# Hybrid decoder layer with a top-4-of-32 MoE on one core: the order of the first expert passes, of their routing, and of the last store of the head

## Chip, core and metric

One core of one Trainium2 chip. The metric is the device time of one execution in microseconds (us), median over the timed runs.

## What is computed

A decoder layer for 512 prompt tokens and 8 sample tokens (520 rows of 1,024), in fp32: attention and a pooling mixer with their projections, then a mixture of experts. The part that matters here:

```python
logits = (h @ w_router + b_router)
topv, topi = lax.top_k(logits, TOP_K)          # 4 of 32
gates = jax.nn.softmax(topv, axis=-1)
# per expert, for the tokens that chose it:
gu = xb @ w1[e] + b1[e]                        # 1024 x 2048
gate, up = gu[:, :D_FF], gu[:, D_FF:]
gate = jnp.minimum(gate, SWIGLU_LIMIT)
up = jnp.clip(up, -SWIGLU_LIMIT, SWIGLU_LIMIT)
act = (up + 1) * (gate * jax.nn.sigmoid(SWIGLU_ALPHA * gate))
out = act @ w2[e] + b2[e]                      # 1024 x 1024
# out * gate is added to the token's row; y = x + gate_ffn * sum
```

All 32 experts are used, so all of w1 and w2 (32 x 12 MB) pass from HBM once.

## The kernel before, in words

**Two parts.** `head` (L399) computes the mixers, the norm, the router's logits, the four choices of each token, each token's place in its experts' lists (`posm`) and the gates (`found`). A barrier of all engines (L358) ends it. `experts` (L1666) then runs 32 *passes*, one expert each, with a class from `ORDER` (L49): A handles 256 tokens, B 128, C 64, D 32. Experts are given to passes by rank of their token counts; passes 0 and 1 are pinned to experts 0 and 1 (class C), so that their weights can be loaded before ranking is known. What does not fit is left to *extra passes* at the end. A and B split fp32 into a high part (ScalarE, L1958) and a low part (VectorE, L2138), with three products each; C and D use fp32 products on 64- or 32-column tiles of the array.

**Weight units and the ring.** A pass has 12 units of 1 MB: 8 of the first matrix, u = 0 to 7 ("up"), 4 of the second, u = 8 to 11 ("down"). SyncE loads units in the order `LOADS` (L89) into a ring of 13 slots (`RING`), and units (1,1) to (1,4), the *early* units, to places of their own. From the 14th load on, each waits until TensorE has used (`unit_used`) the unit that had the slot (L1773). `pe_order` (L74) gives TensorE's order: up of pass 0, down of 0, up of 1, up of 2, down of 1, up of 3, down of 2 and so on; in an A pass the down of the pass before comes after four ups. `LOADS` is the same order without the early units, pass 0 first.

**Rows of a pass.** For pass p: GpSimd copies the expert's columns (`pick_static`, L1817 and L1818), VectorE compares them with slot numbers (`one_hot`, L2070 or L2066), TensorE multiplies (`find_slots`, five small bf16 products into bank 6), VectorE makes the indices (`indices`, L2089 to L2093), GpSimd gathers rows of h by indirect DMA (L1841), TensorE turns them (`turn_rows`, L2331, bank 6), ScalarE copies them out (L1912). In steady state this is done one to three passes ahead.

**Start of the experts.** VectorE's program is: one-hot and indices of pass 0, `gates` (L2208 to L2214), `ranks` (L2166 to L2174, which gives the experts of passes 2 to 31 as `eid`), memsets, one-hot and indices of pass 1, one-hot of pass 2, `extra_passes` (L2178 to L2202), then the passes. GpSimd waits for `eid` before it copies the columns of passes 1, 2 and 3, and gathers pass 1's rows after that. TensorE turns the rows of pass 1 after pass 0's up units, then the activations of pass 0, then `down(0)`. After an up, VectorE clamps banks 0 and 1 (L2100, L2102; `gu_free`) before TensorE may write the biases of the next up.

**End of the head.** Tiles are handled in the order 0, 1, 2, samples (TP), 3. For each, h is stored to DRAM (SyncE L626 for the first three, ScalarE L954 for the last two), turned by TensorE (`turn_h2`, L1606), multiplied with the router (L1616), and VectorE picks the four experts. TensorE waits for tile 3's h before `turn_h2(3)`. SyncE loads units (0,7) to (0,10) once the output projection is done (`xo_ready`), then (1,0) and (1,1); it ends with a wait for all stores of h (L640), and the barrier waits for it. The rest of the early units is loaded by `experts`.

Touched, by line: `pe_order` L74, `SLOT` L90, `behind` L338, SyncE's loads L631 to L637, TensorE's end of the head L1651 to L1664, SyncE's ring wait L1767, GpSimd's start L1859 to L1869, ScalarE's and VectorE's loops over passes, TensorE's `find_slots`, `turn_rows` and its loop.

## Time and profile before

| | us |
|---|---|
| median of 3 runs (1419.0 to 1425.48) | 1425.12 |
| the profiled execution | 1425.26 |
| its span, first to last instruction | 1423.7 |
| TensorE busy (matmul) | 1239.1 (87%) |
| VectorE busy | 668.5 (47%) |
| ScalarE busy | 490.2 (34%) |
| GpSimd busy | 216.3 (15%) |
| DMA: 481.23 MB, mean over the span | 338 GB/s |

All times of rows are us from the span's start. A slice of the page is 35.6 us. The granted clock of TensorE (PEclk) is 1.00 at 2.4 GHz and 0.50 at 1.2 GHz. The DMA share is the mean busy share of the core's 16 DMA engines; it can read slightly over 1. A C unit is 8 matmul records (4 products), and a busy matmul record's end is modelled, so starts are the better measure.

### The profile page before, as it was taken

Reading aid. Unit: us, or ns where it says so; the run is one execution under the profiler, and the core shown is the slowest. Engines: PE = TensorE matmul, PEld = TensorE weight load, DVE = VectorE, ACT = ScalarE, POOL = GpSimd, SP = SyncE. Lnnn points to the kernel's source line nnn. Section 1 sums busy time; section 2 is a strip of 40 time slices with the busy share of each in tenths; the row PEclk is TensorE's granted clock in tenths of the full one; section 3 lists DMA queues with packets and bytes.
Section 4 is the critical chain, followed back from the end, with each engine's and each line's share of the span. In section 5 each row is a group of like instructions: output and inputs, shape, how many; then the busy total and the mean of one; then the engine's idle time right before and its main releaser. Section 6 shows DMA issues by size and latency. Waiting matters only on the chain.

```text
span 1423.7 us, 17364 instructions
## 1 busy us (share of the span) xinstructions
PE 1239.1 (87%) x6405; PEld 729.7 (51%) x6405; DVE 668.5 (47%) x969; ACT 490.2 (34%) x703; POOL 216.3 (15%) x285
## 2 busy tenths in 40 slices
PE   5798777986899998899899969999879999999771
PEld 2353435542267564666575427556447555647330
DVE  2531562355378564353585225427334435848313
ACT  5010431231156443233464213225323333727310
POOL 2211321021101111110211102011201021101001
PEclk9799878996999999899999999999989999999975
DMA  9940585438889999999999999999999999999994
GB/s 289 383 119 5 192 286 201 173 128 324 334 309 390 375 403 397 392 396 355 376 411 406 403 391 396 395 354 405 404 388 405 367 346 408 407 410 405 413 393 187
DMA packets 113657, 481.23 MB, mean 338 GB/s; under 512 B 12497, under 2 KB 13824, under 8 KB 83820
## 3 DMA queue, kind: packets, MB, share of 16 engines
q1 hardware_dynamic: 100460, 451.52, 80.3%
q0 software_dynamic: 12768, 27.47, 7.3%
q8 instruction: 52, 0.85, 0.2%
q10 hardware_dynamic: 344, 1.12, 0.2%
q14 instruction: 33, 0.27, 0.0%
HBM read 463.46 MB, written 24.14 MB: 343 GB/s over the span
## 4 chain that ended last, share of the span: by engine, by line
PE 51%; DMA 13%; SPq 5%; DVE 5%; issue 2%; ACT 1%; POOLq 0%; DVEq 0%; ACTq 0%
PE bank L2305 49%; DMA raw<-in_w 10%; SPq L525 3%; DVE rawr L2138 1%; PE bank L2354 1%; DMA yd<-ost,slot_tok 1%; DMA yd<-gu,slot_tok 1%; SPq L531 1%; PE bank L2331 1%; ACT hi L1958 1%; SPq L535 1%; DVE gu L2102 1%; DVE gu L2100 0%; DVE yf L2298 0%; DVE yf L2295 0%
## 5 line engine op out<-in xcount | busy, mean ns | idle before, releaser
L2138 DVE TENSOR_TENSOR rawr<-raw,hi 128x1024 fp32r<-128x1024 f32 x288 | 341.2, 1220 | 137.7 <-ACT hi L1958 134.7
L1958 ACT CAST hi<-raw 128x1024 fp32r<-128x1024 f32 x288 | 295.2, 1049 | 167.0 <-PE bank L2305 117.5
L2305 PE MATMUL bank<-raw,xT_even 128*64 128x512 f32 (+1 forms) x704 | 139.5, 615 | 4.9 <-DMA raw<-in_w 4.9
L2305 PE MATMUL bank<-raw,aT 128*32 128x256 f32 (+1 forms) x992 | 116.4, 485 | 15.4 <-DMA raw<-in_w 15.4
L1853 POOL DMA_INDIRECT yd<-ost,slot_tok x31 | 54.4, 1754 | 356.3 <-ACT ost L1941 356.0
L2305 PE MATMUL bank<-raw,xT_odd 128*32 128x512 f32 (+1 forms) x544 | 88.6, 677 | 21.5 <-DMA raw<-in_w 21.5
L2305 PE MATMUL bank<-hi,xTh_even 128*128 128x512 f32 x256 | 85.1, 415 | 7.5 <-DVE rawr L2138 7.5
L2305 PE MATMUL bank<-hi,aTh 128*128 128x512 f32 x240 | 77.5, 405 | 9.7 <-DVE rawr L2138 9.7
L2305 PEld LDWEIGHTS bank<-raw,aT 128*32 128x32 f32 (+1 forms) x992 | 42.3, 126 | 79.3 <-issue 41.7
L2305 PE MATMUL bank<-rawr,xTh_even 128*128 128x512 f32 x256 | 81.7, 401 | 0.0
L2305 PE MATMUL bank<-hi,xTl_even 128*128 128x512 f32 x256 | 81.2, 399 | 0.0
L2305 PE MATMUL bank<-hi,xTh_odd 128*128 128x512 f32 x224 | 73.2, 408 | 7.0 <-DVE rawr L2138 7.0
L2305 PE MATMUL bank<-rawr,aTh 128*128 128x512 f32 x240 | 76.0, 399 | 0.0
L2305 PE MATMUL bank<-hi,aTl 128*128 128x512 f32 x240 | 75.6, 397 | 0.0
L1926 ACT ACTIVATE gu<-gu 128x512 f32<-128x512 f32 (+1 forms) x50 | 29.1, 583 | 134.9 <-DVE gu L2100 134.9
L2100 DVE TENSOR_SCALAR gu<-bank 128x512 f32<-128x512 f32 (+1 forms) x50 | 31.3, 627 | 94.0 <-PE bank L2305 94.0
L2305 PEld LDWEIGHTS bank<-raw,xT_even 128*64 128x64 f32 (+1 forms) x704 | 35.7, 128 | 69.7 <-issue 58.9
L2305 PE MATMUL bank<-rawr,xTh_odd 128*128 128x512 f32 x224 | 70.2, 395 | 0.0
L2305 PE MATMUL bank<-hi,xTl_odd 128*128 128x512 f32 x224 | 69.9, 394 | 0.0
L2156 DVE SCALAR_TENSOR_TENSOR aTl<-bank,aTh 128x512 fp32r<-128x512 f32 x30 | 20.7, 689 | 100.6 <-ACT aTh L1919 100.6
L1941 ACT ACTIVATE ost<-bank,slot_gate 128x512 f32<-128x512 f32 (+1 forms) x43 | 26.0, 633 | 120.9 <-PE bank L2305 107.6
L2089 DVE TENSOR_REDUCE slot_raw<-bank 128x1 f32<-128x2 f32 (+1 forms) x32 | 5.0, 156 | 126.4 <-PE bank L2305 125.4
(358 smaller groups left out, 1730.1 us busy)
## 6 DMA issues: line engine op xcount, KB each, us to landing
raw<-in_w SPq DMA_DIRECT2D x356, 1024.0 KB, 17.4
raw<-in_w_ada SPq DMA_DIRECT2D x24, 1024.0 KB, 6.0
raw<-in_w SPq DMA_DIRECT2D x48, 512.0 KB, 11.5
w_in_sb<-in_w_in SPq DMA_DIRECT2D x1, 5120.0 KB
w_out_sb<-in_w_out SPq DMA_DIRECT2D x4, 1024.0 KB, 6.2
early<-in_w SPq DMA_DIRECT2D x4, 1024.0 KB, 8.3
xs<-in_x_prompt SPq DMA_DIRECT2D x4, 512.0 KB, 15.7
yd<-zero POOLq DMA_DIRECT2D x4, 512.0 KB, 10.9
```

Source lines behind the costliest of these rows:

```text
L525: sp.dma_start(raw.rearrange("p (k n) -> p k n", k=2), src).then_inc(landed, 16)
L531: sp.dma_start(raw[:, kk * D:(kk + 1) * D].rearrange("p (h c) -> p h c", h=2), src[:, :, j * 512:(j + 1) * 512]).then_inc(landed, 16)
L535: sp.dma_start(raw, src).then_inc(landed, 16)
L1853: gp.indirect_dma_start(yd_of[n], bass.IndirectOffsetOnAxis(ap=m.slot_tok[:, p % 6, b:b + 1], axis=0), out_rows(p, b), None, bounds_check= ...
L1926: nc.scalar.activation(gate, gate, ACT.Silu, scale=ALPHA).then_inc(silu_ready, 1)
L1941: done = nc.scalar.activation(out_rows(p, b)[:, n * w:(n + 1) * w], src, ACT.Copy, scale=m.slot_gate[:, p % 6, b:b + 1])
L1958: nc.scalar.copy(m.hi[:, (2 * n + h) % HI, :], m.raw[:, slot, h * D:(h + 1) * D]).then_inc(hi_done, 1)
L2100: v.tensor_scalar(gate, g, LIMIT, None, ALU.min).then_inc(gmin_ready, 1)
L2102: v.tensor_scalar(up, u, LIMIT, -LIMIT, ALU.min, ALU.max).then_inc(gu_free, 1)
L2138: v.tensor_tensor(m.rawr[slot][:, half], m.raw[:, slot, half], m.hi[:, (2 * n + h) % HI, :].bitcast(F32), ALU.subtract).then_inc(lo_done, 1)
L2156: v.scalar_tensor_tensor(m.aTl[:, k:k + n, :].rearrange("p k n -> p (k n)"), bank[7][:, 0:n * P], 1.0 / ALPHA, m.aTh[:, k:k + n, :].bitcas ...
L2305: return nc.tensor.matmul(out, lhsT, rhs, start=start, stop=stop, skip_group_check=True)
```

## The change

`pe_order` changes for the first passes: up of 0, up of 1, down of 0, up of 2, down of 1. The order of loads stays; a slot is now freed in TensorE's order (`FREED`), so that the 14th to 25th loads wait for other units than before. Pass 1 becomes an ordinary pass in all programs: pass 0's activations are turned within it, and the search of pass 2 moves to after pass 0's third unit, the rows of pass 1 to after its fifth. GpSimd picks the columns of pass 1, whose expert is known, gathers its rows and loads its biases ahead of the wait for `eid`. VectorE makes one-hot and indices of pass 1 ahead of `ranks`, with half of a memset, and does `extra_passes` in pass 6; its buffer `behind` moves. TensorE does 9 products of the identity with itself after the search of pass 1 and 20 before `turn_h2(3)`; both go to banks that nothing reads. SyncE loads (0,9) and (0,10) only when tile 3's h has been turned, which is after ScalarE has issued its last stores.

```diff
--- before.py
+++ after.py
@@ -76,18 +76,19 @@
     units = []
     for p in range(NE + 1):
         up = [(p, u) for u in range(W1_UNITS)] if p < NE else []
-        down = [(p - 1, u) for u in range(W1_UNITS, UNITS)] if p > 1 else []
-        if not p:
-            down = [(0, u) for u in range(W1_UNITS, UNITS)]
+        down = [(p - 1, u) for u in range(W1_UNITS, UNITS)] if p else []
         cut = 4 if p < NE and ORDER[p] == "A" else W1_UNITS
-        units += up[:cut] + down + up[cut:] if p else up + down
+        units += up[:cut] + down + up[cut:]
     return units
 
 
 USED = {unit: n + 1 for n, unit in enumerate(pe_order())}
 EARLY = [(1, u) for u in range(1, 5)]
 LOADS = [(0, u) for u in range(UNITS)] + [unit for unit in pe_order() if unit[0] and unit not in EARLY]
-SLOT = {unit: n % RING for n, unit in enumerate(LOADS)}
+FREED = [unit for unit in pe_order() if unit not in EARLY]
+SLOT = {unit: n for n, unit in enumerate(LOADS[:RING])}
+for after, unit in zip(FREED, LOADS[RING:]):
+    SLOT[unit] = SLOT[after]
 ALL_USED = NE * UNITS
 SPLIT_UNITS = [unit for unit in pe_order() if ORDER[unit[0]] in SPLIT]
 NTH = {unit: n for n, unit in enumerate(SPLIT_UNITS)}
@@ -335,7 +336,7 @@
         m.eid = ot("eid", [P, NE + EXTRAS + 1], I32)
         m.warm = ot("warm", [P, 1])
         m.cmp = at("cmp", [P, NE, NE], F32, aT0)
-        m.behind = at("behind", [P, EXTRAS, NE], F32, aT0)
+        m.behind = at("behind", [P, EXTRAS, NE], F32, x0 + KC * P * 4)
         m.begun = at("begun", [P, EXTRAS, NE], F32, aT0 + 4096)
         m.yf = at("yf", [P, TP, D], F32, raw0)
         m.yfs = at("yfs", [D // NS // 2, P], F32, raw0 + TP * 4096)
@@ -629,11 +630,13 @@
             for t in TURN[:3]:
                 store_rows(t)
             sp.wait_ge(s.xo_ready, TT)
-            for u in range(7, UNITS - 1):
+            for u in range(7, 9):
+                load_unit(sp, 0, 0, u)
+            sp.wait_ge(s.h2_tr, 2 * TT)
+            for u in range(9, UNITS - 1):
                 load_unit(sp, 0, 0, u)
             sp.wait_ge(m.x1_out, 3 * 16)
             load_unit(sp, 1, 1, 0)
-            sp.wait_ge(s.h2_ready, TT)
             load_unit(sp, 1, *EARLY[0])
             sp.wait_ge(s.ulast_out, 16)
             sp.wait_ge(h2_free[0], 3 * 16)
@@ -1653,6 +1656,8 @@
             positions(1)
             positions(2)
             router(TP)
+            for _ in range(20):
+                mm(bank[4][:, 0:P], m.ident[:], m.ident[:], start=True, stop=True)
             turn_h2(3)
             positions(TP)
             router(3)
@@ -1764,7 +1769,7 @@
                 if p >= PINNED and not u:
                     e[p] = sp.value_load(m.eid[0:1, p:p + 1], min_val=0, max_val=NE - 1)
                 if n >= RING:
-                    sp.wait_ge(unit_used, USED[LOADS[n - RING]])
+                    sp.wait_ge(unit_used, USED[FREED[n - RING]])
                 m.load_unit(sp, e[p], p, u)
 
             def load_extra(x):
@@ -1859,13 +1864,16 @@
             bias(0)
             gp.wait_ge(xg_init, 1)
             gather(0)
+            gp.wait_ge(gates_ready, 1)
+            experts_of[1] = 1
+            pick(1, 1)
+            gp.wait_ge(xg_init, 2)
+            gather(1)
+            bias(1)
             gp.wait_ge(eid_ready, 1)
-            gp.wait_ge(gates_ready, 1)
-            for p in range(1, 4):
+            for p in range(2, 4):
                 pick_static(p)
             gp.wait_ge(xg_init, 3)
-            gather(1)
-            bias(1)
             for p in range(NE + 2):
                 if p:
                     bias(p + 1)
@@ -1996,24 +2004,15 @@
                         swish(c, h, HB[p])
                     continue
                 high_to(USED[p, 1] + 2)
-                if p > 1:
-                    last_act(p - 1, 0)
+                last_act(p - 1, 0)
                 high_to(USED[p, 3] + 2)
-                if p > 1:
-                    last_act(p - 1, 1)
+                last_act(p - 1, 1)
                 for g in range(4):
                     high_to(USED[p, 4 + g] + 2)
-                    if p:
-                        static_x(p + 1, g)
-                if not p:
-                    static_x(1, 0)
+                    static_x(p + 1, g)
                 for h in range(HALVES[c]):
                     swish(c, h, HB[p])
-                if not p:
-                    last_act(0, 0)
-                    last_act(0, 1)
-                    gated(0)
-                if p > 1:
+                if p:
                     high_to(USED[p - 1, UNITS - 1] + 2)
                     gated(p - 1)
             last_act(NE - 1, 0)
@@ -2217,16 +2216,16 @@
             v.memset(m.xg[0][:, 0, 0:512], 0.0).then_inc(xg_init, 1)
             indices(0)
             gates()
+            v.memset(m.xg[1][:, 0, 0:512], 0.0).then_inc(xg_init, 1)
             v.wait_ge(i_done, 2)
             v.tensor_reduce(m.slot_gate[:, 0, 0:1], bank[6][:, 8:11].unsqueeze(1), AX_X, ALU.add).then_inc(gates_ready, 1)
+            one_hot(1)
+            indices(1)
             ranks()
-            v.memset(m.xg[1][:], 0.0).then_inc(xg_init, 1)
+            v.memset(m.xg[1][:, 0, 512:D], 0.0)
             v.memset(m.xg[0][:, 0, 512:D], 0.0)
             v.memset(m.xg[0][:, 1, :], 0.0).then_inc(xg_init, 1)
-            one_hot(1)
-            indices(1)
             one_hot(2)
-            extra_passes()
             for p in range(NE):
                 c = ORDER[p]
                 if c == "A":
@@ -2248,26 +2247,20 @@
                     swiglu(p, 2, USED[p, 7])
                     continue
                 low_to(USED[p, 1] + 2)
-                if p > 1:
-                    last_act(p - 1, 0)
+                last_act(p - 1, 0)
                 low_to(USED[p, 2] + 1)
                 indices(p + 2)
                 low_to(USED[p, 3] + 1)
-                if p > 1:
-                    last_act(p - 1, 1)
+                last_act(p - 1, 1)
                 low_to(USED[p, 4] + 1)
                 for g in range(4):
                     low_to(USED[p, 4 + g] + 1)
-                    if p:
-                        low_x(p + 1, g)
+                    low_x(p + 1, g)
                     if not g:
                         one_hot(p + 3)
-                if not p:
-                    low_x(1, 0)
                 swiglu(p, 0, USED[p, 7])
-                if not p:
-                    last_act(0, 0)
-                    last_act(0, 1)
+                if p == ORDER.index("A") - 2:
+                    extra_passes()
             low_to(ALL_USED)
             last_act(NE - 1, 0)
             last_act(NE - 1, 1)
@@ -2316,11 +2309,9 @@
 
                 if p < NE:
                     pe.wait_ge(oh_ready, p + 1)
-                    if p:
-                        pe.wait_ge(x_ev, HB[max(p - 1, 1)])
-                        pe.wait_ge(xl_done, SB[max(p - 1, 1)])
-                    if p == 2:
-                        pe.wait_ge(idx_ready, 2)
+                    if p > 1:
+                        pe.wait_ge(x_ev, HB[p - 1])
+                        pe.wait_ge(xl_done, SB[p - 1])
                     find(ORDER[p], m.pb[:, p % 4] if p else m.found[:, 0], 5 if p else 2)
 
             def turn_x(c, g, xg):
@@ -2336,7 +2327,7 @@
                 if p < NE and g < HALVES[ORDER[p]]:
                     if not g:
                         pe.wait_ge(xg_in[p % 2], GATHERED[p])
-                        pe.wait_ge(idx_ready, min(p + 2, NE) if p else 1)
+                        pe.wait_ge(idx_ready, min(p + 2, NE))
                     else:
                         pe.wait_ge(x_ev, HB[p] + g)
                         if ORDER[p] in SPLIT:
@@ -2501,9 +2492,14 @@
                     last = mm(bank[6][:, 8:11], m.oh[:, t, 0:P], m.found[:, 0, t, 2:5], start=not t, stop=t == TP)
                 last.then_inc(i_done, 1)
 
+            def keep_busy(n):
+                for _ in range(n):
+                    mm(bank[7][:, 0:P], m.ident[:], m.ident[:], start=True, stop=True)
+
             find_slots(0)
             find_gates()
-            pe.wait_ge(gates_ready, 2)
+            find_slots(1)
+            keep_busy(9)
             turn_rows(0, 0)
             for p in range(NE):
                 c = ORDER[p]
@@ -2537,22 +2533,15 @@
                     continue
                 for u in range(W1_UNITS):
                     up_static(p, u)
-                    if u == 1 and p > 1:
+                    if u == 1:
                         turn_last_act(p - 1, 0)
-                    if u == 3 and p > 1:
+                    if u == 3:
                         turn_last_act(p - 1, 1)
                     if u == 2:
-                        find_slots(p + 2 if p else 1)
-                    if u == 4 and not p:
-                        find_slots(2)
-                    if u >= 4 and p:
+                        find_slots(p + 2)
+                    if u >= 4:
                         turn_rows(p + 1, u - 4)
-                if not p:
-                    turn_rows(1, 0)
-                    turn_last_act(0, 0)
-                    turn_last_act(0, 1)
-                    down(0)
-                elif p > 1:
+                if p:
                     down(p - 1)
             turn_last_act(NE - 1, 0)
             turn_last_act(NE - 1, 1)
```

## Rows read from the trace of the kernel before

**Rows 1.** The page's slices (40 of 35.6 us), DMA busy in tenths.

```profile
DMA  9940585438889999999999999999999999999994
```

**Rows 2.** Windows: stretch, length, busy us by engine, TensorE clock, DMA share, GB/s.

```profile
338.00:348.00 10.00, 8.89 (x28) 3.35 (x30) 4.99 (x7) 0.58 (x1) 2.32 (x6) 0.60 0.29 100
348.00:366.00 18.00, 12.07 (x65) 4.35 (x61) 13.81 (x38) 1.78 (x3) 4.72 (x8) 0.92 1.01 416
366.00:374.00 8.00, 8.00 (x29) 2.59 (x31) 0.00 (x0) 0.00 (x0) 0.00 (x0) 0.76 0.60 226
384.00:403.00 19.00, 17.28 (x66) 9.77 (x63) 11.00 (x12) 8.61 (x10) 2.04 (x3) 0.82 0.67 230
403.00:480.00 77.00, 75.61 (x352) 50.37 (x352) 53.29 (x63) 42.50 (x50) 9.79 (x11) 1.00 0.98 365
```

**Rows 3.** SyncE's timeline, 344 to 352: its first loads into the ring after the wait.

```profile
344.99 6.56 SPq L535 DMA_DIRECT2D raw<-in_w  x4
```

**Rows 4.** Timeline of TensorE, 318 to 400: start, length, group, [idle before it].

```profile
318.32 1.97 PE L1606 MATMUL bank<-ident,h 128*128 128x128 f32 x8 [4.67 <-DVE h L1302]
320.96 3.62 PE L1616 MATMUL bank<-w_router_sb,h2T 128*128 128x32 f32 x16 [0.57 <-ACT h2T L947]
339.11 1.08 PE L2331 MATMUL bank<-ident,xg_even 128*128 128x128 f32 x4 [5.83 <-issue]
340.12 1.22 PE L2305 MATMUL bank<-bt,sel_sb 12*128 12x512 f32 x2
341.27 7.66 PE L2305 MATMUL bank<-raw,xT_even 128*64 128x512 f32 x24
361.41 0.63 PE L2331 MATMUL bank<-ident,xg_odd 128*128 128x128 f32 x4 [3.17 <-DVE slot_tok L2093]
381.38 3.65 PE L2305 MATMUL bank<-early,xT_odd 128*64 128x512 f32 x16
393.37 1.74 PE L2305 MATMUL bank<-bt,sel_row 12*128 12x512 f32 x4 [1.72 <-DVE gu L2102]
```

**Rows 5.** Timeline of TensorE, 296 to 319, at the full clock.

```profile
298.10 5.40 PE L1582 MATMUL bank<-w_out_sb,mixT 128*128 128x512 f32 x12
303.33 1.04 PE L1606 MATMUL bank<-ident,h 128*128 128x128 f32 x8
307.64 1.87 PE L1616 MATMUL bank<-w_router_sb,h2T 128*128 128x32 f32 x16
```

**Rows 6.** VectorE's last step of the head; SyncE's wait; stores of h (KB, us to landing).

```profile
327.23 0.21 DVE L1279 RECIPROCAL gsum<-gsum 8x1 f32<-8x1 f32 x2
SPq L640 <- DMA h2d<-h: 8.5, 1, 8.5
h2d<-h SPq DMA_DIRECT2D x3, 512.0 KB, 5.7
h2d<-h ACTq DMA_DIRECT2D x1, 512.0 KB, 8.9
```

**Rows 7.** Timelines of VectorE and GpSimd, 339 to 361.

```profile
339.89 0.18 DVE L2174 CAST eid<-ex 128x32 int32<-128x32 f32 x1
342.67 0.76 DVE L2070 TENSOR_TENSOR oh<-pcol,rows_sb 128x640 bf16<-128x640 f32 x1
350.27 0.09 DVE L2178 MEMSET zero_e<- 128x32 f32 x1
360.79 0.15 DVE L2202 CAST eid<-ends 128x1 int32<-128x1 f32 x1
341.90 1.57 POOL L1817 COPY pcol<-posm 128x5 f32 x1 [0.47 <-issue]
```

**Rows 8.** TensorE's waits, 560 to 582 (us, times, longest); VectorE's timeline in pass 6.

```profile
PE bank L2305 <- DMA raw<-in_w: 7.2, 6, 1.9
PE bank L2305 <- DVE rawr L2138: 2.0, 1, 2.0
544.07 4.62 DVE L2138 TENSOR_TENSOR rawr<-raw,hi 128x1024 fp32r<-128x1024 f32 x4
```


## Prediction

> **What bounds the kernel now.** Read the slices first: DMA is at nine tenths or more in nearly all of the expert phase [rows 1]; 1 MB weight units (1.05 million bytes) come at 416 GB/s in an undisturbed stretch, 2.52 us each [rows 2]. So the end is set by when the weight stream starts and by every stretch in which it stands still before the passes that wait for weights; where TensorE itself waits again, at 560 to 582 us, six of its waits, 7.2 us, are for weights [rows 8]. Then read the stage windows for those still stretches [rows 2]: width times (1 minus share) gives 7.1 us at 338 to 348, 3.2 at 366 to 374, 6.3 at 384 to 403, and 1.5 over 403 to 480. The first is the wait for the first use of a weight: the ring of 13 slots and the 4 early units are full, and the first load after them is issued at 344.99, when unit (0,0) has been used [rows 3]. The others are a full ring too, since TensorE is what stops: it uses a C unit in 1.8 us (two units, 16 records, in 3.65), faster than weights come, but sits idle 3.2 us for the rows of pass 1, whose indices stand behind the extra-pass arithmetic in VectorE's program, then turns the activations and restarts cold [rows 4, 7].
>
> **The sum**, against the profiled execution's 1425.26 us (span 1423.7; the median of the runs is 1425.12, practically the same).
>
> *1. End of the head.* Tile 3's chain is transposes 1.97 us and router 3.62 us, both at the half clock [rows 4]; at full clock the same groups take 1.04 and 1.87 [rows 5]. The 20 identity products stand in the 4.67 us in front [rows 4]. No row shows a 128-column fp32 product. Bounds: 0.23 us (router, 32 columns, 1.87/8) and 0.90 (512 columns, 5.40/6) [rows 5]; I take 0.24, nearest the narrow one, so 20 take 4.8 us, about the wait. If they hold the clock, 0.9 + 1.75 = 2.7 us go; at 0.37 each they run 2.7 us over and the gain is nil. The expert phase starts only when tile 3's store has landed, too: SyncE waits 8.5 us for it, it lands 8.9 us after its issue at 318.3, the first three in 5.7 [rows 6]. The store now has two weight units ahead of it in place of five: I take 5.7, landing at 324.0. VectorE's last step moves from 327.4 [rows 6] to 324.7; both are early enough, so 2.7 us. If the store kept 8.9 it would land at 327.2 and the gain would be 0.2. The Trainium skill (DMA: Bandwidth & Descriptors, Queues, rings and completion order) says that each DMA engine takes turns between queues packet by packet. ScalarE's queue would then not stand behind SyncE's weights at all, the reordering would free nothing, and with 0.2 here the sum below would be 2.5 higher; 8.9 beside 5.7 speaks against that. The delayed units, (0,9) and (0,10), leave DMA idle some 2 us at 318; they aren't used before pass 0's second matrix, and the stream of the first 17 units then ends near 340.5 rather than 339.1.
>
> *2. First use.* TensorE turns pass 0's rows at 339.11 after 5.83 us of idleness [rows 4]; the landing shifts by 2.7, to 336.4. Into the idle stretch go pass 1's copies, one-hot (0.76 us [rows 7]) and search, some 1.9 us together, then 9 products, at the cold router's 0.45 each (3.62/8) 4.1 us: 6.0 against 5.83. So they cost nearly nothing by themselves; at twice that price they would be 4 us late and take all of this step. If the clock is up, the transposes and biases lose about half of 1.08 and 1.22 us, on the path 0.8, and the first three units, 7.66 us where 5.5 would do, lose 1.9 in unit (0,0). First use: 344.99 - 2.7 - 2.7 = 339.6 warm, 342.3 cold. I take 340.6, one late, since GpSimd's copy for pass 1 now runs beside a memset, and such a copy took 1.57 us [rows 7]. [...] The stream restarts **4.4 us** earlier (2.7 to 5.4).
>
> *3. Between pass 0 and pass 1.* The extra-pass arithmetic (350.27 to 360.9 [rows 7]) leaves the path, and pass 0's second matrix goes behind pass 1's first. Early units free no slot, so the tenth load after the restart waits for unit (1,5). TensorE from first use to there: 13 units at 1.8 = 23.4, three groups of transposes at 0.63 = 1.9, two searches of five small products, an estimate of 0.2 each beside the 0.63 of four transposes, = 0.4, biases 0.6, and a new wait: pass 1's biases need VectorE's two limits of pass 0, 1.7 us by the row of the same wait before pass 2 [rows 4]. Queued behind it are all of pass 1's units; SyncE waits for those. Sum 28.0 us. DMA in that time: 9 units at 2.52 (416 GB/s) and pass 2's rows (0.5 MB, 1.3 us): 24.0. Still stretch: 4.0 us. Then 7 units (17.6 us) are freed by TensorE in 6 units and biases, some 13 us, so none before pass 2. That replaces 3.2 + 6.3 = 9.5: **5.5 us** gained. If the clock falls in the 1.7 us wait, two units at the half clock take 3.6 of it.
>
> *4. Passes 2 and 3.* From unit (2,0) on both kernels free and load in the same order. The DMA now has a backlog of 2 to 4 us there: of 1.5 idle I take **1.2**, between 0 and 1.5.
>
> *5. Hidden.* Ranking ended at 340.1 [rows 7] and moves behind one-hot and indices of pass 1, some 1.7 us, and forward by 2.7: 339.1; three memsets (1.9 us) and pass 2's one-hot follow by 342, and its search is due after three units, at 344. GpSimd's bias and gather of pass 1 only move forward. SyncE's first expert-dependent load is the fourth after the ring. The extra-pass work, 10.6 us, now stands in pass 6 ahead of VectorE's last four low halves at 544.07 [rows 8]: unit (5,10) waits some 9.9 us. Behind it TensorE has 7.2 us of waits for weights and 2.0 for VectorE that can shrink [rows 8], plus the 2 to 5 us by which it leads DMA more than before. Cost taken: none.
>
> Sum: 4.4 + 5.5 + 1.2 = 11.1; 1425.3 - 11.1 = **1414.2 us**.
>
> **Rivals.**
> *A, the clock stays down at both places:* the first use is 2 us earlier, the still stretch is 4.0 + 3.6 = 7.6, and nothing is left for passes 2 and 3: 2.0 + 1.9 + 0 = 3.9, so **1421.4**. For: the half clock lasted through the transposes and biases after 339.11. Against: the wait in the head is nearly filled.
> *B, partly given back:* the pass 6 wait restarts TensorE cold, 9.9 + 3.6 = 13.5, against 9.2 of waits to absorb it; 4.3 reaches pass 8, which then ends later with a full ring: 1414.2 + 4.3 = **1418.5**.
> *C, slower:* the same place, if nothing of the 13.5 is absorbed because weights of pass 7 and the A pass stop behind a full ring, with A's 3.9 as the only gain: 1425.3 + 13.5 - 3.9 = **1434.9**. It decides from the point where the A pass starts over 4 us late (A) or over 11 (forecast). Against: weights are what TensorE waits for behind this place, and an empty ring of 13 units is 33 us of transfer.
> *D, the change doesn't do what it says:* pass 1's rows or pass 2's slots come late and TensorE stops after unit (0,2) or (0,3). The margin is 2 us; 5 us late, 3 over it, makes **1417.2**.
>
> **How the numbers follow.** Forecast 0.68, A 0.13, B 0.09, D 0.05, C 0.05. Best bounds together: 5.4 + 7.2 (a new wait hidden) + 1.5 = 14.1, 1411.2; the runs of before spread over 6 us, so the low end goes 3 further, to 1408. The high end takes in D, B and A: 1421.5. About 0.5%, 7 us, is what a measurement here can tell from none: faster needs under 1418.0. The forecast and D are faster: 0.73; A and B are the same: 0.22; C is slower: 0.05.
>
> **What would show it.** Expert phase about 2.7 us earlier, router(3) near 1.9 us; first load after the ring near 340.6; no transposes of pass 1 after pass 0 but within it; still stretches of DMA near 340 and 365, of 2 and 4 us, and none at 395; VectorE's extra-pass steps in pass 6 with TensorE idle up to 10 us beside them. Wrong if the still stretches after the restart stay near 9.5 us, or if those of the A passes (640 to 700) grow by what was won.

## The result

| | before | after |
|---|---|---|
| median of 4 runs, us | 1422.06 (1417.87 to 1425.48) | 1406.34 (1398.94 to 1407.76) |
| profiled execution, us | 1425.26 | 1407.76 |
| its span, us | 1423.7 | 1406.1 |

The ratio is 0.9886, 95% interval 0.9857 to 0.9914: faster by 1.1%. The direction and the places are those of the prediction; the size is not: 15.7 us by the medians (17.6 by the spans of the two profiles) against 11.1 forecast. The median lies 1.7 us below the range's low end, 1408; that it lies outside hangs on the base as well, since the kernel before has a median of 1422.06 here and the forecast counted from 1425.3: the same 15.7 us taken off that would be 1409.6, inside.

To compare profiles one needs a common start, since unchanged code ahead of the change shifts from one execution to the next. I count from SyncE's issue of unit (0,7), just ahead of the first thing that the change moves. Here it is in SyncE's timeline of the kernel before, then of the kernel after (start us, us over which the group was issued, line, operation, count):

```profile
311.34 0.33 SPq L535 DMA_DIRECT2D raw<-in_w  x1
```

```profile
309.76 0.33 SPq L536 DMA_DIRECT2D raw<-in_w  x1
```

So 1.6 us of the profiles' difference were there before the change begins. From here on, "at 28.5" means 28.5 us behind this issue.

**The head.** TensorE's timeline of the kernel after (start us, us, group, idle before it), the answer to [rows 4] up to the barrier:

```profile
312.01 4.73 PE L1660 MATMUL bank<-ident 128*128 128x128 f32 x40
318.79 2.15 PE L1619 MATMUL bank<-w_router_sb,h2T 128*128 128x32 f32 x16
```

The 20 products (40 records) took 4.73 us, 0.24 each, and fill the old wait of 4.67 us; transposes (1.09) and router take 3.2 us in place of 5.6. VectorE ends the head at 323.80; its first step of the experts, with the wait for the barrier ahead of it:

```profile
325.52 0.83 DVE L2069 TENSOR_TENSOR oh<-posm,rows_sb 128x640 bf16<-128x640 f32 x1 [1.71 <-PEq L359]
```

**The first use.** TensorE again, from the nine products to the wait between the passes:

```profile
330.81 3.81 PE L2298 MATMUL bank<-ident 128*128 128x128 f32 x18
334.84 0.66 PE L2322 MATMUL bank<-ident,xg_even 128*128 128x128 f32 x4 [0.22 <-DMA xg_even<-h2d,slot_tok]
336.23 5.37 PE L2298 MATMUL bank<-raw,xT_even 128*64 128x512 f32 x24
352.77 0.69 PE L2298 MATMUL bank<-bt,sel_sb 12*128 12x512 f32 x2 [1.48 <-DVE gu L2101]
353.39 2.57 PE L2298 MATMUL bank<-raw,xT_odd 128*64 128x512 f32 x8
355.74 3.00 PE L2298 MATMUL bank<-early,xT_odd 128*64 128x512 f32 x8
```

The rows land 0.22 us after the nine products end, transposes and the first three units run at the full clock (5.37 where [rows 4] has 7.66), and TensorE doesn't stop until pass 1's biases, where it waits 1.48 us for VectorE's limits. Behind that wait the clock does fall (0.73 granted at 352.7 to 359): two units take 5.57 us, where at the full clock they take 3.83 (e9 below).

SyncE's timeline of the kernel after: the first load into a freed slot, and the load into the slot that unit (2,0) frees:

```profile
338.21 32.20 SPq L536 DMA_DIRECT2D raw<-in_w  x11
...
383.31 0.35 SPq L536 DMA_DIRECT2D raw<-in_w  x1
```

The first is at 28.5 against 33.7 before [rows 3], 5.2 us earlier. The same two of the kernel before are at 344.99 [rows 3] and here:

```profile
400.70 3.15 SPq L535 DMA_DIRECT2D raw<-in_w  x2
```

That is 89.4 behind the issue of (0,7) before, and 73.5 after: **15.8 us earlier**, practically the whole gain of the medians (the best bounds of the prediction together made 14.1).

**The DMA.** Windows of the kernel after (stretch, length, busy us by engine, clock, DMA share, GB/s), the answer to [rows 2]:

```profile
338.00:350.00 12.00, 12.00 (x63) 4.17 (x61) 3.70 (x8) 0.58 (x1) 4.08 (x10) 1.00 1.00 391
360.00:373.00 13.00, 13.00 (x66) 4.41 (x64) 3.81 (x8) 1.78 (x4) 1.32 (x2) 1.00 0.72 268
373.00:384.00 11.00, 11.00 (x51) 5.63 (x48) 6.38 (x6) 6.36 (x8) 2.31 (x4) 1.00 0.97 388
384.00:403.00 19.00, 18.43 (x91) 14.65 (x90) 15.49 (x18) 12.21 (x14) 1.80 (x1) 1.00 1.02 416
403.00:480.00 77.00, 76.18 (x346) 48.03 (x344) 54.65 (x63) 44.28 (x50) 8.56 (x11) 1.00 1.00 386
```

The 7.1 us at 338 to 348 are gone, one still stretch (width times 1 minus share, as in the prediction) of 13 x 0.28 = 3.6 us is left at 360 to 373 (4.0 forecast), and the one at 384 to 403 is gone. Summed as in the prediction, the kernel before stood still 11.0 us from its first load to 480, this one 3.9 (3.6 and 11 x 0.03): 7.1 less, and the forecast said 6.7. By this measure the prediction was right; yet the load freed by (2,0) gained 15.8 - 5.2 = 10.6 us over the same stretch. The measure is what has to be looked at.

**Pass 6.** TensorE's waits of the kernel after, 500 to 600 (us, times, longest), against [rows 8]:

```profile
PE bank L2298 <- DVE rawr L2137: 9.6, 1, 9.6
```

The extra-pass arithmetic costs a wait of 9.6 us (9.9 forecast), and all the waits for weights, 7.2 us before, are gone.

### The profile page after: what moved, and what is told of

Its sections match the earlier page's. It is cut to its first block, busy times and chain, and to the rows that moved or that the text cites. A ratio compares the mean times of both kernels' runs of the same rounds, so it can differ in the third digit from the quotient of the medians.

```text
span 1406.1 us, 17471 instructions
## 1 busy us (share of the span) xinstructions
PE 1237.9 (88%) x6463; PEld 732.5 (52%) x6463; DVE 670.0 (48%) x970; ACT 490.2 (35%) x703; POOL 215.4 (15%) x285
## 4 chain that ended last, share of the span: by engine, by line
PE 54%; DMA 12%; DVE 5%; SPq 3%; issue 1%; ACT 1%; POOLq 0%; ACTq 0%; DVEq 0%
PE bank L2298 51%; DMA raw<-in_w 9%; SPq L526 3%; DVE rawr L2137 2%; PE bank L2345 1%; DMA yd<-ost,slot_tok 1%; PE bank L2322 1%; DMA yd<-gu,slot_tok 1%; ACT hi L1966 1%; DVE gu L2101 1%; SPq L532 1%; DMA xg_even<-h2d,slot_tok 0%; DVE gu L2099 0%; DVE yf L2291 0%; DVE yf L2288 0%
## 5 line engine op out<-in xcount | busy, mean ns | idle before, releaser
L2298 PE MATMUL bank<-hi,aTh 128*128 128x512 f32 x240 | 78.5, 409 | 17.8 <-DVE rawr L2137 17.8
L2298 PEld LDWEIGHTS bank<-hi,aTh 128*128 128x128 f32 x240 | 45.1, 194 | 33.8 <-DVE rawr L2137 22.5
## 6 DMA issues: line engine op xcount, KB each, us to landing
yd<-zero POOLq DMA_DIRECT2D x4, 512.0 KB, 10.6
```

The lines of the kernel that those rows point to most:

```text
L2298: return nc.tensor.matmul(out, lhsT, rhs, start=start, stop=stop, skip_group_check=True)
```

## The experiments

Two theories. **Theory 1:** what counts is the time that TensorE itself takes up to a point where the ring is full and the DMA waits for it, first unit (2,0); what the DMA did before is forgotten there. **Theory 2**, the prediction's measure: the DMA's still stretches add up to the end. Two of the expectations name a Theory 3 too: the passes of class A take up about 4 us of any delay, and what is over goes through to the end. The table gives for every kernel the ratio of its time to the kernel before's, and from its one profile the issue of the load freed by (2,0) and the time at which the DMA has moved 100 MB since the issue of (0,7), both counted from that issue. A single profile's end scatters by some 4 us either way after that, so positions in the stream tell more than ends.

| kernel | ratio (95%) | (2,0) | 100 MB |
|---|---|---|---|
| before | 1 | 89.4 | 275.9 |
| after | 0.9886 (0.9857 to 0.9914) | 73.5 | 259.7 |
| f1, before + the order | 0.9978 (0.9954 to 1.0003) | 84.1 | 270.1 |
| f2, after - the order | 0.9928 (0.9904 to 0.9951) | 81.9 | 268.1 |
| e4, extra passes ahead | 0.9953 (0.9926 to 0.998) | 81.3 | 267.2 |
| e3, extra passes in pass 1 | 0.9886 (0.9858 to 0.9913) | 73.7 | 259.7 |
| e1, no products | 0.9889 (0.9864 to 0.9914) | 77.4 | 263.2 |
| e9, no twenty | 0.9881 (0.9848 to 0.9914) | 74.1 | 260.0 |
| e10, no nine | 0.9882 (0.9849 to 0.9915) | 74.8 | 260.7 |
| e2, old store order | 0.9885 (0.9859 to 0.991) | 74.7 | 260.7 |
| g1, ring loads late | 0.9884 (0.985 to 0.9918) | 73.8 | 259.8 |
| e6, 15 products before pass 2 | 0.9889 (0.9865 to 0.9912) | 75.4 | 261.6 |
| e12, 40 products before pass 2 | 0.9939 (0.9913 to 0.9966) | 81.0 | 267.3 |
| h1, 40 products before pass 4 | 0.9945 (0.9921 to 0.9969) | 73.7 | 267.8 |
| g2, 6 products, extras in pass 1 | 0.9887 (0.986 to 0.9915) | 73.2 | 259.6 |
| h2, 6 products | 0.9859 (0.9825 to 0.9893) | 72.0 | 258.4 |

In fifteen of the sixteen the two columns differ by 185.8 to 186.6 us; the one exception is h1, which delays TensorE between them.

### Which part brings it

f1 is the kernel before with the new order of units and slots alone, f2 the changed kernel with the old order, everything else kept.

```diff
-        down = [(p - 1, u) for u in range(W1_UNITS, UNITS)] if p > 1 else []
-        if not p:
-            down = [(0, u) for u in range(W1_UNITS, UNITS)]
+        down = [(p - 1, u) for u in range(W1_UNITS, UNITS)] if p else []
...
-        units += up[:cut] + down + up[cut:] if p else up + down
+        units += up[:cut] + down + up[cut:]
...
-                    sp.wait_ge(unit_used, USED[LOADS[n - RING]])
+                    sp.wait_ge(unit_used, USED[FREED[n - RING]])
```

> The kernel before with the new order of units and slots alone (up 0, up 1, down 0); rows of pass 1, extra passes, store and clock as before. Theory 1 (TensorE's time at the first unit of pass 2 carries to the end): TensorE still stops for rows and activations after pass 0, but the wait and the half clock ahead of pass 2 (1.7 us and about 3 us) go: the load freed by (2,0) 4 to 6 us earlier than before, and the end too: ratio 0.996 to 0.997. Theory 2 (DMA's still stretches): the tenth load now waits for (1,5), some 12 us of stillness in place of 11 in several pieces: ratio 0.999 to 1.002.

> The kernel before with everything of the change except the order of units: products, store, rows of pass 1 ahead of ranking, extra passes in pass 6. Theory 1: first load of the ring 5 to 6 us earlier counted from the issue of (0,7), the 3.2 us wait for rows gone, most of the half clock after it too, so the load freed by (2,0) 11 to 13 us earlier, and the end with it: ratio 0.991 to 0.992. Theory 2 (my sum by still stretches: 4.4 us for the start, 3 for the rows): 7 to 8 us, ratio 0.9945 to 0.995.

The order alone moves (2,0) by 5.3 us, everything but the order by 7.4; together 15.8. That is 3.1 us more than the two, but it doesn't show that they exist only with both. f2 has the changed kernel's TensorE program up to the first units, and its profile has them at the half clock (0.50 granted from 329.8 to 339; the changed kernel is at the full clock from 334 on). TensorE's timeline of f2, pass 0's first three units:

```profile
336.05 7.00 PE L2314 MATMUL bank<-raw,xT_even 128*64 128x512 f32 x24
```

They take 5.37 in the changed kernel. So f2's first load into a freed slot comes at 31.1 instead of 28.5, 2.7 us late by the clock alone. With these given back f2 moves (2,0) by some 10.1 us (an estimate), and the two parts practically add up. The times agree: f2's ratio of 0.9928 is 10.2 us, and its profiled execution is 4 us above its median. Neither expectation of f2 came as it stood. Its position, 7.4 us, is theory 2's number (theory 1 had 11 to 13), its ratio lies between the two theories' ratios, and the interval reaches both. f1's position lies in theory 1's 4 to 6 us, while its interval reaches both theories' ratios. These two runs split the change, then, and don't decide between the theories.

TensorE's waits of f1 between 341 and 394 say why the order alone gets so little:

```profile
PE bank L2331 <- DVE slot_tok L2093: 3.2, 1, 3.2
PE bank L2354 <- DVE gu L2109: 2.1, 1, 2.1
```

The rows of pass 1 are still late and pass 0's activations are still turned at once. The extra passes weigh about as much as the order, which f2 lacks (8.4 us later than the changed kernel at (2,0), 2.7 of them clock). e4 puts them back ahead of pass 0 in VectorE's program, e3 puts them into pass 1:

```diff
             one_hot(2)
+            extra_passes()
...
-                if p == ORDER.index("A") - 2:
-                    extra_passes()
```

> The changed kernel with the extra-pass arithmetic back ahead of pass 0's work on VectorE. Indices of pass 2 come 10 us later, TensorE waits some 6 to 7 us for them inside pass 0 and loses clock; the 9.6 us wait in pass 6 goes. Theory 1: the load freed by (2,0) 7 us later than in the changed kernel, end 7 us later, ratio 0.9935. Theory 3: 3 to 4 us later, ratio 0.991. Theory 2: DMA has loads queued during that wait for pass 0's freed slots only, still stretch of 3 to 5 us more, ratio 0.991 to 0.992.

> The changed kernel with the extra-pass arithmetic in pass 1, where VectorE is idle for 8 us, in place of pass 6. Theory 1: the 9.6 us wait of TensorE in pass 6 goes, TensorE then waits for weights in pass 7 instead, and the A pass starts no more than 1 us earlier, so the end is within 1 us of the changed kernel (ratio 0.988 to 0.9886). Rival B of the prediction (part of the wait reached the A pass): 2 to 5 us faster, ratio 0.985 to 0.987.

The longest of e4's waits of TensorE, 338 to 393:

```profile
PE bank L2321 <- DVE slot_tok L2092: 6.3, 1, 6.3
```

The indices of a pass come 6.3 us late and (2,0) is 7.7 later, near theory 1's 7; the ratio is 0.9953 (0.9935 forecast, inside the interval). In e3 nothing of the early stream changes, and TensorE's main waits at 500 to 600 are these:

```profile
PE bank L2298 <- DMA raw<-in_w: 5.0, 5, 1.9
PE bank L2298 <- DVE rawr L2137: 2.5, 1, 2.5
```

Without the 9.6 us wait TensorE simply waits for weights again, the ratio is the same 0.9886, and 100 MB arrive at the same 259.7. The wait in pass 6 costs nothing that these runs can see: shown, not only argued. What no run leaves out by itself is the early picking of pass 1's rows, so its share of the gain isn't known.

### The head

e1 leaves out all 29 products, e9 the 20, e10 the nine; e2 loads (0,9) and (0,10) again with (0,7), ahead of the last store:

```diff
-            for _ in range(20):
-                mm(bank[4][:, 0:P], m.ident[:], m.ident[:], start=True, stop=True)
...
-            keep_busy(9)
```

```diff
-            for u in range(7, 9):
-                load_unit(sp, 0, 0, u)
-            sp.wait_ge(s.h2_tr, 2 * TT)
-            for u in range(9, UNITS - 1):
+            for u in range(7, UNITS - 1):
                 load_unit(sp, 0, 0, u)
...
             load_unit(sp, 1, 1, 0)
+            sp.wait_ge(s.h2_ready, TT)
             load_unit(sp, 1, *EARLY[0])
```

The last lines bring back the old wait of unit (1,1) for tile 3's h, so that it too is loaded as before.

> The changed kernel without its 29 identity products. Theory 1 (TensorE's time at the first unit of pass 2 passes whole to the end): the head ends about 1.5 to 2 us later after the issue of unit (0,7), the first load of the ring 4 to 5 us later (half clock in transposes, biases and unit (0,0)), the load that unit (2,0) frees as much later, and so the end: about 5 us slower than the changed kernel, ratio to the kernel before 0.992. Theory 2 (only DMA's still stretches count, as I predicted): the still stretch at the first use grows by 3 to 4 us and the one in pass 1 stays, so 3 to 4 us slower, ratio 0.991; the two differ in whether the end moves as much as the load freed by (2,0).

> Without the 20 products ahead of the rows' transposes, with the nine kept. Theory 1: transposes and router run at half clock again, the first operation of the experts comes 2.1 us later behind the issue of unit (0,7) (17.8 instead of 15.7), the load freed by (2,0) at 76 instead of 73.5, ratio 0.990. Rival: the nine alone suffice (the head has slack elsewhere): issue at 73.5, ratio 0.9886.

> Without the nine products ahead of the first pass, with the twenty kept. Theory 1: the first two expert units run at half clock, the first load into a freed slot comes 2.8 us later, the load freed by (2,0) at 76.3 instead of 73.5, ratio 0.9905. Rival: the clock holds from the router's work across the wait, or the loss is taken up in the wait between passes 0 and 1: issue at 73.5, ratio 0.9886.

> The changed kernel with units (0,9) and (0,10) loaded with (0,7) again, ahead of the last store. Theory 1 (the store's landing holds the barrier): h lands some 2.5 us later, about 8.5 us after its issue, the barrier moves from VectorE's last step to that landing, 2 to 2.5 us later, and the end with it: ratio 0.990. Rival (queues take turns packet by packet, so the weights of the other queue hardly matter): the landing moves by under 0.5 us and so does the end: ratio 0.9886.

The barrier lets the experts start at 15.8 in the changed kernel, at 17.8 without the twenty (e1, e9), at 17.8 with the old order of the store (e2), and at 17.8 before. Either part alone gives nothing there: each removes one of two things that end at nearly the same time. The store itself, in the DMA issues of 300 to 340 of the changed kernel and then of e2 (KB, us from issue to landing):

```profile
h2d<-h ACTq DMA_DIRECT2D x1, 512.0 KB, 3.0
```

```profile
h2d<-h ACTq DMA_DIRECT2D x1, 512.0 KB, 8.9
```

The time to landing is 3.0 us with two weight units issued ahead of it and 8.9 with five ([rows 6] has 8.9 too). The forecast took 5.7. The two units were in fact through: in either kernel the DMA moves 2.1 to 2.2 MB from the issue of (0,7) to that of the store, which is two units. In the changed kernel the DMA is half idle then (share 0.55 at 316.7 to 318.5), in e2 it isn't (1.06): three of the five units are still to come, and the store lands only when the DMA has moved 3.4 MB more, about these three and the store.

Yet none of the four loses more than 3.8 us at (2,0): e9 0.6, e10 1.2, e2 1.1, e1 3.8, where the expectations of e9 and e10 had 2.5 to 2.8 each. e9's units behind the wait between the passes show where it goes:

```profile
357.91 0.70 PE L2296 MATMUL bank<-bt,sel_sb 12*128 12x512 f32 x2 [1.48 <-DVE gu L2099]
358.54 1.94 PE L2296 MATMUL bank<-raw,xT_odd 128*64 128x512 f32 x8
360.31 1.89 PE L2296 MATMUL bank<-early,xT_odd 128*64 128x512 f32 x8
```

The wait is 1.48 us as in the changed kernel, but here the clock stays up (1.94 and 1.89 for 2.57 and 3.00), and 1.7 us come back. In ten profiles, TensorE's program being the same from the first unit to well behind this wait, the clock fell behind it in four (after, e3, g1, h1) and held in six (e1, e2, e6, e9, e10, e12). It is not all chance: the nine products took 3.62 to 3.81 us in the four in which it fell, so that it had risen early in them, and 3.99 to 4.19 in those of the six that have them. So each part's worth read from one profile is uncertain by 1.7 us (and f2's by 2.7 at the first use). e9, e10, e2 and e1 corrected by it lose 2.3, 2.9, 2.8 and 5.5 us at (2,0), near the 2 to 2.8, and 4 to 5 for e1, that were expected. In the times none of it shows: the four ratios, 0.9881 to 0.9889, are the changed kernel's 0.9886 within intervals of some 4 us either way, where 0.990 to 0.992 were expected. What the products and the store's order bring is shown by position alone.

### TensorE's time or the DMA's still stretches

g1 makes SyncE's first nine loads into freed slots wait for two more units, so the DMA loses time early while TensorE does not:

```diff
-                    sp.wait_ge(unit_used, USED[FREED[n - RING]])
+                    sp.wait_ge(unit_used, USED[FREED[n - RING]] + (2 if n < RING + 9 else 0))
```

> SyncE's first nine loads into a freed ring slot each wait for two more units to be used, some 3.5 us later; TensorE's own work is untouched. Counted from the issue of unit (0,7), the load freed by unit (2,0) is issued at 73.5 us in the changed kernel, and 100 MB have arrived at 259.7. Theory 1 (TensorE's time at unit (2,0) alone sets the stream behind it, the DMA's still stretches ahead of it don't count): the still time ahead of it grows by 3 to 4 us, the issue stays at 73.5 +- 1, and the ratio at 0.9886 (0.987 to 0.990). Theory 2 (the still stretches add up, as the prediction had it): everything behind comes 3.6 us later, the ratio is 0.991.

g1's SyncE timeline and its windows:

```profile
341.11 28.77 SPq L536 DMA_DIRECT2D raw<-in_w  x11
...
382.77 0.35 SPq L536 DMA_DIRECT2D raw<-in_w  x1
```

```profile
340.00:362.00 22.00, 20.52 (x96) 6.76 (x94) 3.78 (x11) 1.81 (x3) 3.38 (x9) 0.92 0.91 357
362.00:374.00 12.00, 12.00 (x57) 4.05 (x55) 4.63 (x7) 3.31 (x5) 1.19 (x2) 1.00 0.95 366
```

The first load is at 32.1 instead of 28.5, 3.7 us late; the still stretch at 362 to 374 shrinks in turn (share 0.95, in the changed kernel 0.70), and (2,0) is at 73.8 for 73.5. What the DMA loses early it would have lost at the full ring anyway. I had expected the still time to grow; it moved. The issue, the 100 MB and the ratio are theory 1's, and theory 2's 3.6 us did not come. What fails is theory 2 as a forecast, which takes an early still stretch as lost for good; counted afterwards, the sum of still stretches is no larger than in the changed kernel.

The opposite test delays TensorE. e6 and e12 put 15 and 40 products in front of pass 2's biases, h1 puts 40 in front of pass 4's (e12's edit is shown; e6 has 15 in it, h1 p == 4):

```diff
                 bias = m.bt[:, p % BIAS_BUFS, :]
+                if p == 2:
+                    keep_busy(40)
                 up_bias(c, 0, bias)
```

> The changed kernel with 15 identity products (3.6 us at the full clock) on TensorE ahead of the biases of pass 2. Theory 1 (TensorE's time at unit (2,0) passes whole to the end): the load freed by (2,0) comes 3.6 us later, every later load of passes 3 to 6 too, and the end as well: 3.6 us slower, ratio 0.991. Theory 2 (DMA's still stretches count): DMA has some 5 us of loads queued at that point, so nothing but 0 to 1 us reaches the end: ratio 0.9886 to 0.9893.

> The changed kernel with 40 identity products (9.5 us) ahead of the biases of pass 2; 15 of them left the end unchanged within its interval. Theory 3 (a slack of about 4 us is absorbed at the A passes, beyond it TensorE's time carries through): end 5 to 6 us later than the changed kernel, ratio 0.992 to 0.993. Theory 1: 9.5 us later, ratio 0.995. Theory 2: DMA has 5 us queued, so 4 to 5 us, ratio 0.992, but then with still stretches of DMA between 385 and 400.

> Forty products of the identity, 9.2 us, in TensorE's program ahead of pass 4's biases (450.6 in the changed kernel), well behind unit (2,0). The load freed by (2,0) stays at 73.5 us behind the issue of unit (0,7) either way. Theory 1a (only TensorE's time up to (2,0) sets the stream): 100 MB at 259.7 as in the changed kernel, ratio 0.9886. Theory 1b (TensorE's time sets the stream wherever the ring is full, and it is full once more at 440 to 450, where the DMA stands still for 0.8 us): 100 MB some 7 to 9 us later, at 267 to 269, ratio 0.994 to 0.995.

e12's products take 9.20 us; (2,0) moves by 7.4, and the clock behind the wait of pass 1, which held there, accounts for the 1.8 between (e6: 3.5 us of products by the same price, moved by 1.8). Against h2 below, in which the clock held as well, (2,0) moves by 9.0 us for 9.2 of products and by 3.4 for 3.5: a delay ahead of (2,0) is paid there nearly one to one. It reaches 100 MB whole, 7.6 us later in e12. That is too much for theory 2's 4 to 5 and theory 3's 5 to 6. The end fits (e12's median is 7.4 us above the changed kernel's), but the interval of the ratio, 0.9913 to 0.9966, would allow all three, and e6's ratio, 0.9889, tells nothing apart. In h1, TensorE's timeline and the window of that place:

```profile
453.26 9.09 PE L2298 MATMUL bank<-ident 128*128 128x128 f32 x80
```

```profile
452.00:470.00 18.00, 18.00 (x126) 12.71 (x126) 1.10 (x4) 1.86 (x3) 1.99 (x4) 1.00 0.65 218
```

Forecast were two ends: nothing, if only the time up to (2,0) counts, or 7 to 9 us, if every full ring counts. It is the second: 100 MB come 8.1 us later, the ratio is 0.9945. The ring is full again near 450 (the kernel after moves 324 GB/s at 440 to 450.6), and the DMA's share falls to 0.65 while the products run. But 9.6 us lost in pass 6, 100 us further on, cost nothing, since there TensorE is ahead of its weights (without the wait it waits for weights, e3). So theory 1, in the form that these runs bear out: **TensorE's time counts between full rings; a delay is free only where it stands in place of a wait for weights.**

### The half clock that was left

g2 and h2 put six products ahead of pass 1's biases, to fill the 1.48 us; g2 also does the extra passes in pass 1.

```diff
+                if p == 1:
+                    keep_busy(6)
                 if p:
                     pe.wait_ge(gu_free, HB[p])
```

> Six products of the identity ahead of the biases of pass 1, and the arithmetic of the extra passes beside it in pass 1 instead of pass 6. In the changed kernel the steps at 353 to 359 us run at half clock behind the wait between passes 0 and 1 (2.57 and 3.00 us where full clock has about 1.4). Theory 1: if that half clock goes, unit (2,0) comes 1.5 to 1.8 us earlier and the whole stream with it: load freed by (2,0) at 72.0 instead of 73.5 us behind the issue of unit (0,7), ratio 0.9875, which an interval hardly tells from 0.9886. Theory 2 (the still stretches of the DMA count, not TensorE's time): they are 5.4 us in all there, so the gain is at most the same 1.5 us, none if the DMA was busy meanwhile. If the clock is low all the same: no change.

> The six products ahead of pass 1's biases alone, with the extra passes left in pass 6, where VectorE has nothing in front of the indices of pass 3. Theory 1 (TensorE's time up to (2,0) is the stream's): the half clock at 353 to 359 goes, and no wait of 1.05 us at 364 takes its place; the load freed by (2,0) at 72.0 +- 0.3 us behind the issue of unit (0,7) against 73.5, 100 MB at 258.2. Rival: the DMA, nine tenths busy there, gives nothing more: 73.5. The ratio would be 0.9875 or 0.9886, which the interval doesn't tell apart; the trace does.

TensorE's timeline of h2:

```profile
351.49 1.61 PE L2298 MATMUL bank<-ident 128*128 128x128 f32 x12
...
353.68 1.94 PE L2298 MATMUL bank<-raw,xT_odd 128*64 128x512 f32 x8
355.45 1.89 PE L2298 MATMUL bank<-early,xT_odd 128*64 128x512 f32 x8
```

In g2 the half clock went, but (2,0) came only 0.3 us earlier, not the 1.5 to 1.8 expected, because a new wait took its place:

```profile
363.88 0.63 PE L2322 MATMUL bank<-ident,xg_even 128*128 128x128 f32 x4 [1.05 <-DVE slot_tok L2092]
```

VectorE's indices of pass 3 stood behind the extra passes. With these left in pass 6 (h2), TensorE has no wait from 338 to 385 and (2,0) is at 72.0, as forecast, 1.5 us earlier, and 100 MB come 1.3 us earlier: again TensorE's time is the stream's. h2's ratio is 0.9859 (0.9825 to 0.9893); the intervals of the two kernels overlap widely, so that h2 is faster than the changed kernel is what its trace says and its time does not yet show.

## Why the prediction was wrong, and where it was right

*What bounds the kernel* failed in its first sentence on the sum: "the end is set by when the weight stream starts and by every stretch in which it stands still". The still stretches were forecast well, and they are the wrong thing to add. A full ring makes the DMA wait for TensorE, and at that moment the stream's time is TensorE's time. From the first load to the load freed by (2,0), windows of the kernel before and of the kernel after:

```profile
344.99:400.70 55.71, 48.06 (x204) 18.89 (x201) 23.99 (x52) 9.22 (x13) 8.35 (x13) 0.87 0.84 323
```

```profile
338.21:383.31 45.10, 43.62 (x199) 16.16 (x196) 15.02 (x25) 9.26 (x13) 7.70 (x15) 0.96 0.91 361
```

TensorE is 10.6 us sooner there. The still time by shares falls only from 0.16 x 55.7 = 8.9 to 0.09 x 45.1 = 4.1 us, by 4.8. Most of what lacks is a backlog: the DMA has moved 18.0 MB before and 16.3 after, so 1.7 MB, 4.1 us at 416 GB/s, are issued and still to come. The next 58.2 us of both:

```profile
400.70:458.90 58.20, 57.63 (x267) 41.60 (x266) 45.92 (x52) 37.46 (x41) 6.74 (x7) 1.00 0.96 366
```

```profile
383.31:441.51 58.20, 57.63 (x267) 41.63 (x266) 46.87 (x53) 37.47 (x41) 6.74 (x7) 1.00 1.01 406
```

TensorE does the same work in the same 57.63 us, and the changed kernel moves 58.2 x 40 GB/s = 2.3 MB more, the backlog: it is made up while TensorE's time passes, and costs and gains almost nothing (100 MB come 186.5 us behind the load freed by (2,0) before, 186.2 after). The share, 0.96 and 1.01, makes 3 us of the stream's time out of what is 5.6 by bytes, so it also tells lost time too small; why was not tried.

*Step 1, end of the head, 2.7 us:* 2.1 came. Products, transposes and VectorE were as forecast (0.24 us a product; 1.09 for 1.04; router 2.15 for 1.87, its last part at a falling clock: 1.00 granted at 318.5 to 320, 0.72 at 320 to 321). The store was better than the 5.7 taken: 3.0. The Trainium skill (DMA: Bandwidth & Descriptors, Queues, rings and completion order) has each DMA engine take turns between queues packet by packet. That would let the store pass the waiting weights, and the traces don't bear it out: with three units still to come it landed behind about all of them, 8.9 us after its issue, and without the reordering the barrier falls back by 2.0 us. Step and rival price were right; that the reordering is indispensable to the products' 2 us was in the prediction as its 0.2, and e2 shows it.

*Step 2, first use, 1.7 us beyond step 1:* 3.1 came, so 5.2 for both against 4.4 forecast and a warm bound of 5.4. GpSimd's copy, for which I had taken one microsecond of delay, took 0.19 us. From GpSimd's timeline of the kernel after this copy and a later one, and from VectorE's the instruction beside the later one:

```profile
329.36 0.19 POOL L1822 COPY pcol<-posm 128x5 f32<-128x5 f32 x1 [0.18 <-DVE found L2213]
...
339.82 1.05 POOL L1822 COPY pcol<-posm 128x5 f32 x1 [0.47 <-issue]
```

```profile
340.06 0.76 DVE L2065 TENSOR_TENSOR oh<-pcol,rows_sb 128x640 bf16<-128x640 f32 x1
```

My reading of [rows 7] was wrong: the memset is not what makes such a copy long. VectorE's memset of pass 1's rows runs from 329.21 to 329.69, beside the copy of 0.19 us. The long copies, 1.57 us before and 1.05 after, overlap the one-hot comparison as well and end 0.04 us behind its end (343.47 against 343.43, 340.87 against 340.82), in every profile of this case. The Trainium skill (SBUF — State Buffer, Who interferes with whom) says that a VectorE instruction with two inputs in SBUF contends with a GpSimd instruction that reads SBUF; both of the comparison's inputs are there, and the traces agree. On the path of pass 1's rows there is no such comparison beside the copy.

*Steps 3 and 4, 5.5 + 1.2 = 6.7 us:* this is the step that failed. It subtracted the DMA's 24.0 us from TensorE's 28.0, counted the 4.0 that were left as the still stretch and set that against the still stretches before, 9.5. What came is 10.6, TensorE's own time saved. TensorE's waits of the kernel before between the first load and (2,0), 344 to 401:

```profile
PE bank L2331 <- DVE slot_tok L2093: 3.2, 1, 3.2
PE bank L2354 <- DVE gu L2109: 2.1, 1, 2.1
PE bank L2305 <- DVE gu L2102: 1.7, 1, 1.7
PE bank L2305 <- ACT aT L1919: 0.7, 1, 0.7
```

These are 7.7 us, of which 1.5 are left. The rest is clock: before, the second matrix of pass 0 ran in 8.65 us and (2,0) with its biases at half speed too. From the timeline of the kernel before, then that of the kernel after:

```profile
366.62 8.65 PE L2305 MATMUL bank<-raw,aT 128*64 128x512 f32 x32
...
395.05 1.22 PE L2305 MATMUL bank<-hi,xTh_even 128*128 128x512 f32 x2
```

```profile
371.98 7.09 PE L2298 MATMUL bank<-raw,aT 128*64 128x512 f32 x32
378.99 1.19 PE L2298 MATMUL bank<-bt,sel_row 12*128 12x512 f32 x4
380.11 0.73 PE L2298 MATMUL bank<-hi,xTh_even 128*128 128x512 f32 x2
```

Waits 6.2, second matrix 1.6, its biases and those of pass 2 (1.74 in [rows 4]) 0.8, the first six groups of products of (2,0) 5.3 - 2.9 = 2.4, transposes 0.5, the rest of pass 0's first units 0.6, minus the 1.7 of half clock behind the new wait: 10.4 of 10.6; 0.2 us I can't place. What the kernel before loses here was in its trace. Summed this way, the same views would have given 4.4 and some 10, 14 to 15 us and a forecast near 1410. I had even priced TensorE from the first use to (1,5), 28.0 us (29.4 in the trace, 27.7 in e6, in which the clock held).

*Step 5, hidden:* right in all parts. Indices of pass 3 and slots of pass 2 were in time, eid was ready at 338.0, which is 339.6 counted from the kernel before's issue of (0,7) (339.1 forecast), the pass 6 wait was 9.6 for 9.9 and cost nothing.

*Rivals.* A's half clock came in the profile of the changed kernel at the second of its two places, for 1.7 us rather than 3.6; f2's profile has it at the first, for 2.7. B and C stood on the pass 6 wait reaching the A passes; e3 rules them out. D, that rows or slots come late, did not occur; e4 and g2 show what it costs: 6.3 and 1.05 us of TensorE. The range's low end failed with the sum: its best bounds, 14.1 us, had the shares' 1.5 us as the most that passes 2 and 3 could give, and had no term for TensorE's half clock at (2,0). That 15.7 us then fell outside, where a base of 1425.3 would have kept it inside, is the scatter of the runs.

## What to carry to other kernels

Where a ring of buffers is full, count the consumer's own time up to the next slot that it frees, waits and half clock included, and not the idle share of the transfers: what the DMA loses in front of a full ring is lost anyway. Then ask, stretch by stretch, which side is ahead: 9.2 us on TensorE cost 9.0 ahead of pass 2 (at an equal clock) and 8.1 ahead of pass 4, and 9.6 us in pass 6, where TensorE waited for weights, cost none, which makes that the place for work that has to be done somewhere. Compare profiles from the last instruction that the change leaves alone; here the head in front of it moved by up to 9 us between executions.

## What was unexpected of the hardware

- A DMA share of 0.96 with 366 GB/s and of 1.01 with 406 in equal stretches of the same work on TensorE: the share falls by a twentieth where the rate falls by a tenth.
- A store of 512 KB on ScalarE's queue landed 3.0 us after its issue when the weight units on SyncE's queue were through, and 8.9 when three of them were still to come. The two queues are not independent here.
- The same wait of 1.48 us between the same instructions let the clock fall to 1.2 GHz in four profiles and not in six, worth 1.7 us. The Trainium skill (TensorE: Matmul & The Clock Gate, Part 1: The HAM clock gate) says that the point at which the clock rises varies from run to run of one kernel. The traces agree (behind the same products it was up at 334 in the changed kernel and only at 339 to 340 in f2), and here the fall behind a wait varies too, so a single profile can't price what fills such a wait. Six products of the identity in it (g2, h2) kept the clock up both times.
- Products of the identity cost 0.24 us each in the twenty, which began at the full clock, and 0.42 in the nine, which began at the half clock after idleness (0.47 in f2, at the half clock throughout).
- A GpSimd copy of 128x5 took 0.19 us beside a VectorE memset and 1.05 us when VectorE's two-input comparison ran beside it.
